# Two-mixer stage of a two-block transformer: row sums as a 129th column, values as weights, attention output in columns

## The chip, the cores and the metric

One core of a Trainium2 chip runs the whole program. The metric is the device time of one execution in microseconds. Engines: PE is TensorE (PEld its weight loads), DVE VectorE, ACT ScalarE, POOL GpSimd, SP SyncE, which here only issues DMAs.

## The reference, cut to what matters

The program computes two transformer blocks on 1024 tokens of width 1024. The change is in the second block, where two mixers run side by side on 8 chunks of 128 tokens: attention over a window of 128 keys (8 heads of 64, 2 key and value heads), and a gated linear recurrence (mlstm, 4 heads of 128).

```python
mx = jnp.maximum(logits.max(axis=-1, keepdims=True), sink)
e = jnp.exp(logits - mx)
p = e / (e.sum(axis=-1, keepdims=True) + jnp.exp(sink - mx))
out = jnp.einsum('bkgnqs,bnskd->bnqkgd', p, vv)          # attention, then
att = rms_norm(out.reshape(b, s, 512), norm_att_out)     # over all 512 columns of a token
...
num = einsum('bhts,bhsd->bhtd', s, v) + a * einsum('bhtk,bhkv->bhtv', q, c_st)
den = s.sum(axis=-1) + a * einsum('bhtk,bhk->bht', q, n_st)
h = num / jnp.maximum(jnp.abs(den), jnp.exp(-m_t))[..., None]
c_new = decay * c_st + einsum('bhsk,bhsv->bhkv', k * w, v)
n_new = decay * n_st + einsum('bhs,bhsk->bhk', w, k)
...
x = x + jnp.concatenate([att, rms_norm(sigmoid(o) * h)], axis=-1) @ w_out
```

## The kernel before, in words

The program is a row of stages, each with its own instruction list per engine, written out by hand and separated by a barrier. `stage_in2` projects the inputs, `stage_mixers` (L1820 to L2270) does both mixers, `stage_residual` multiplies by w_out and adds. Nothing in `stage_mixers` is planned by a scheduler: the order of the calls in each engine's function is the order of its queue, and semaphores join the engines.

`stage_mixers` runs an unrolled loop over 8 blocks i of 128 tokens. PE's part of a block, in its order:

- `h_back(i-1)` (L1999) turns the recurrence's result into columns; `scores(i+1, (0, 1))` (L1895) multiplies queries by keys for four of eight heads.
- `read(i)`: per head two matmuls with a ones column or n_st as the moving operand, 1 column each, for den (L1920, L1921, into bank N), and two with 128 columns for num (L1922, L1923, bank O).
- `memory_project(i-1)` (L1942, L1945): keys and values of the later cross attention, 8 matmuls of 256 columns; it is work of another part of the network, put here.
- `write(i)`: per head a 1-column matmul for the change of n (L1952) and one of 128 columns for the change of the state c (L1953, bank U).
- `scores(i+1, (2, 3))`, then `turn(i)` (L1969): 16 transposes of probabilities in four groups, two banks, each of which DVE copies out (`keep`, L2123) before the third and fourth group.
- `att_back(i-1)` (L1989): 4 transposes of the normed attention rows; `keys(i+1)` (L1909): 4 transposes.
- `weigh(i)` (L1979): probabilities as weights (128x128), values as the moving operand, 64 columns: 16 matmuls. `decays(i+1)` (L1902) ends the block.

Every fp32 matmul shows as two instructions in the trace, a transpose as one. DVE, between its waits, scales the attention rows (L2136), makes m_s (`weights`, L2077), the logits (L2045) and their maxima, `hidden` (L2095 to L2104), the state's update (L2111 to L2116) and `keep`. ACT makes the exponentials (L2190), norms both results (`att_norm`, `h_norm`), and scales by the gains on the way out of the banks (`att_out` L2232, `h_out` L2238):

```python
for h in range(QH):                 # weigh(n), L1979
    kv = h // (QH // 2)
    for r in range(2):
        m = pe.matmul(T[1][:, h * DH:(h + 1) * DH], pt[:, 2 * h + r, :],
                      va[:, n + r, kv * DH:(kv + 1) * DH], start=r == 0, stop=r == 1)
```

SP loads the gate rows of a chunk (L1884), each after an update of the state, and at block 2 the memory rows and both halves of w_ckv (1 MB, 2 MB, 2 MB).

`stage_residual` first loads the stream (4 MB, SP) and then w_out in tiles of 512 KB; ACT (`split_high`, L205) and DVE (`split_low`, L212) split its input into two parts, and `Weights` does so with w_out.

Of the kernel before, what the change touches and what calls it, by code (L numbers as in the profile page):

```python
# [17 lines left out]
ALU = mybir.AluOpType  # L18
# [4 lines left out]
P = 128  # L23
# [30 lines left out]
ML_H = 4  # L54
MEM = 256
# [51 lines left out]
def stage_constants(nc, ctx, A, K, bank):  # L107
# [4 lines left out]
    with ExitStack() as inner:  # L112
# [3 lines left out]
        @block.sync  # L116
        def _(sp):
            sp.wait_ge(rows_zero, 1)
            for name, source, n in VECS:
                a = A[source]  # L120
                v = a.rearrange("o (k p) -> (o k) p", p=P) if len(a.shape) == 2 else a.rearrange("o t (k p) -> (o t k) p", p=P)
                c = VEC[name]
                sp.dma_start(rows[c % P:c % P + n, c // P, :], v).then_inc(rows_in, 16)
            sp.wait_ge(rows_in, 16 * len(VECS))
# [42 lines left out]
        def _(pe):  # L167
            pe.wait_ge(rows_in, 16 * len(VECS))
# [33 lines left out]
def split_high(act, x, xh, made, first=0, end=None):  # L202

    for t in range(first, end or len(x)):
        act.copy(xh[t], x[t]).then_inc(made, 1)  # L205


def split_low(dve, x, xh, xl, hi_made, made):

    for t in range(len(x)):  # L210
        dve.wait_ge(hi_made, t + 1)
        dve.tensor_tensor(xl[t], x[t], xh[t], ALU.subtract).then_inc(made, 1)  # L212


class Weights:
# [4 lines left out]
    def __init__(self, ctx, inner, nc, name, tiles, used):  # L220
# [6 lines left out]
    def load(self, sp, n, s, source):  # L227
        sp.wait_ge(self.lo_made, free(n))
        sp.dma_start(self.raw[:, s, :, :], source).then_inc((self.loaded0, self.loaded1)[s], 16)

    def high(self, act, n, s, round_):
        act.wait_ge((self.loaded0, self.loaded1)[s], 16 * round_ + 16)
# [1293 lines left out]
def stage_in2(nc, ctx, A, K, bank, u, qa, ka, va, qk, vm, og, cols, dist, sinks, rows_d):  # L1526
# [12 lines left out]
    with ExitStack() as inner:  # L1539
# [8 lines left out]
        v_rows, q_rows = vm[0:ML_H, :, :].rearrange("p c n -> p (c n)"), qa[0:ML_H, :, :].rearrange("p k t -> p (k t)")  # L1548
        gi, lf, m_, negm = (v_rows[:, j * SEQ:(j + 1) * SEQ] for j in range(4))
        b, a = (q_rows[:, j * SEQ:(j + 1) * SEQ] for j in range(2))  # L1550
        row2 = q_rows[:, 2 * SEQ:4 * SEQ].rearrange("p (c r t) -> p c r t", r=2, t=P)

# [102 lines left out]
        def _(act):  # L1655
# [19 lines left out]
            def keep_group(n, c):  # L1675
# [5 lines left out]
                else:  # L1681
                    act.copy(vm[:, c, 384:512], out[:, 0:P])
# [51 lines left out]
        def _(dve):  # L1734
# [75 lines left out]
            for c in range(NB):  # L1810
                dve.wait_ge(gmm, NB + c + 1)
                dve.tensor_copy(vm[:, c, 0:384], bank[4 + c % 2][:, 0:384]).then_inc(g_kept, 1)
# [7 lines left out]
def stage_mixers(nc, ctx, A, K, bank, qa, ka, va, qk, vm, og, cols, dist, sinks, rows_d, mk, mv):  # L1820

    (scored, logit, maxed, exped, root, turned, pt_kept, pvmm, small, scaled, ss_made, normed, back, b_kept) = sems(
        ctx, nc, "a", "scored logit maxed exped root turned pt_kept pvmm small scaled ss_made normed back b_kept")
    (bc0, bc1, rm_made, dec, gate_made, fmm, s_made, q_made, kt, kw_made, omm, den_made, hmade, umm, state, nmade,
     hs_made, h2_made, hback, hb_kept, wexp) = sems(
# [1474 lines left out]
```

## Time and profile before

| | |
|---|---|
| median of 3 runs | 3372.41 us (3363.12 to 3375.85) |
| the profiled execution | 3371.22 us, its span 3369.5 us |
| busy share of the span: PE, PEld, DVE, ACT, POOL | 85%, 75%, 48%, 36%, 17% |
| granted PE clock over the span | 0.909 of full speed |
| `stage_mixers` | from about 2025 to 2282 us of the span |

A granted clock of 1.00 is 2.4 GHz, 0.50 is 1.2 GHz; a stretch between them was partly at either level. Busy time of PE and of PEld overlap. A duration of a matmul includes latency, so the pace of a sequence is read from start to start.

### The profile page before, as it was taken

Reading aid. Unit: us, or ns where it says so; the run is one execution under the profiler, and the core shown is the slowest. Engines: PE = TensorE matmul, PEld = TensorE weight load, DVE = VectorE, ACT = ScalarE, POOL = GpSimd, SP = SyncE. Lnnn points to the kernel's source line nnn. Section 1 sums busy time; section 2 is a strip of 40 time slices with the busy share of each in tenths; the row PEclk is TensorE's granted clock in tenths of the full one; section 3 lists DMA queues with packets and bytes.
Section 4 is the critical chain, followed back from the end, with each engine's and each line's share of the span. In section 5 each row is a group of like instructions: output and inputs, shape, how many; then the busy total and the mean of one; then the engine's idle time right before and its main releaser. Section 6 shows DMA issues by size and latency. Waiting matters only on the chain. (4 is left out here: it accounts for less than half of the span.)

```text
span 3369.5 us, 39296 instructions
## 1 busy us (share of the span) xinstructions
PE 2864.1 (85%) x14811; PEld 2515.0 (75%) x14811; DVE 1616.0 (48%) x1956; ACT 1219.2 (36%) x1781; POOL 575.8 (17%) x336
## 2 busy tenths in 40 slices
PE   3889999888499999979939998987677569999992
PEld 2879999788388999867818897775566458888882
DVE  2336655450523323224363415442323369999995
ACT  3324333321311111123233215442221257777773
POOL 2000000003422222101040000002201234444341
PEclk7999999999799999989969997788888589999996
DMA  2332222342121111032211212003001269999995
GB/s 102 107 109 95 95 95 91 113 128 76 50 62 44 50 44 50 25 137 94 94 62 45 46 37 88 19 7 100 25 0 27 119 256 411 407 404 405 405 408 199
DMA packets 223133, 432.17 MB, mean 128 GB/s; under 512 B 21302, under 2 KB 159914, under 8 KB 197690
## 3 DMA queue, kind: packets, MB, share of 16 engines
q1 hardware_dynamic: 213018, 396.21, 32.7%
q0 software_dynamic: 10016, 34.62, 2.6%
q8 instruction: 66, 1.08, 0.1%
q14 instruction: 33, 0.27, 0.0%
HBM read 370.85 MB, written 59.93 MB: 128 GB/s over the span
## 5 line engine op out<-in xcount | busy, mean ns | idle before, releaser
L3050 DVE TENSOR_TENSOR k_w_lo<-k_raw,k_w_hi 128x2048 fp32r<-128x2048 f32 x192 | 435.4, 2291 | 51.0 <-ACT k_w_hi L2996 47.1
L2996 ACT CAST k_w_hi<-k_raw 128x2048 fp32r<-128x2048 f32 x192 | 363.5, 1907 | 94.2 <-PE bank L2916 48.2
L192 PE MATMUL bank<-u_ffn_hi,f_w_hi 128*128 128x342 f32 (+1 forms) x880 | 308.5, 351 | 33.7 <-POOL f_w_lo L1323 33.7
L193 PE MATMUL bank<-u_ffn_lo,f_w_hi 128*128 128x342 f32 (+1 forms) x880 | 308.5, 351 | 0.0
L194 PE MATMUL bank<-u_ffn_hi,f_w_lo 128*128 128x342 f32 (+1 forms) x880 | 308.2, 350 | 0.0
L238 POOL TENSOR_TENSOR wo_w_lo<-wo_w,wo_w_hi 128x1024 fp32r<-128x1024 f32 x16 | 38.3, 2396 | 1371.5 <-ACT wo_w_hi L234 1371.5
L2914 PE MATMUL bank<-k_w_hi,k_x_hi 128*128 128x512 f32 x512 | 206.6, 403 | 5.8 <-DVE k_x_lo L3056 5.6
L192 PEld LDWEIGHTS bank<-u_ffn_hi,f_w_hi 128*128 128x128 f32 x880 | 166.8, 190 | 49.8 <-issue 34.2
L2915 PE MATMUL bank<-k_w_lo,k_x_hi 128*128 128x512 f32 x512 | 203.6, 398 | 0.0
L2916 PE MATMUL bank<-k_w_hi,k_x_lo 128*128 128x512 f32 x512 | 203.3, 397 | 0.0
L192 PE MATMUL bank<-u_hi,g_w_hi 128*128 128x342 f32 (+2 forms) x576 | 190.8, 331 | 13.5 <-DVE g_w_lo L746 10.6
L193 PE MATMUL bank<-u_lo,g_w_hi 128*128 128x342 f32 (+2 forms) x576 | 185.2, 321 | 0.0
L194 PE MATMUL bank<-u_hi,g_w_lo 128*128 128x342 f32 (+2 forms) x576 | 184.2, 320 | 0.0
L194 PEld LDWEIGHTS bank<-u_ffn_hi,f_w_lo 128*128 128x128 f32 x880 | 166.7, 189 | 15.6
L193 PEld LDWEIGHTS bank<-u_ffn_lo,f_w_hi 128*128 128x128 f32 x880 | 166.4, 189 | 15.8
L1323 POOL TENSOR_TENSOR f_w_lo<-f_raw,f_w_hi 128x1024 fp32r<-128x1024 f32 x44 | 105.3, 2395 | 380.9 <-ACT f_w_hi L1349 380.9
L1433 PE MATMUL bank<-d_x_hi,d_w_hi 128*128 128x512 f32 x352 | 138.7, 394 | 23.6 <-DVE d_x_lo L1460 23.3
L1381 DVE TENSOR_SCALAR hidden<-f_gate,vec 128x1024 f32 x22 | 17.9, 812 | 262.0 <-ACT f_gate L1355 262.0
L1434 PE MATMUL bank<-d_x_lo,d_w_hi 128*128 128x512 f32 x352 | 138.3, 393 | 0.0
L1435 PE MATMUL bank<-d_x_hi,d_w_lo 128*128 128x512 f32 x352 | 138.1, 392 | 0.0
L1459 DVE TENSOR_TENSOR d_w_lo<-d_raw,d_w_hi 128x1024 fp32r<-128x1024 f32 x44 | 55.5, 1262 | 169.3 <-ACT d_x_hi L1484 169.3
L192 PEld LDWEIGHTS bank<-u_hi,g_w_hi 128*128 128x128 f32 x576 | 109.3, 190 | 14.1 <-DVE g_w_lo L746 11.0
(538 smaller groups left out, 6982.8 us busy)
## 6 DMA issues: line engine op xcount, KB each, us to landing
k_raw<-in_w_e_gate_dram SPq DMA_DIRECT2D x64, 1024.0 KB, 8.1
k_raw<-in_w_e_up_dram SPq DMA_DIRECT2D x64, 1024.0 KB, 7.5
k_raw<-in_w_e_down_dram SPq DMA_DIRECT2D x64, 1024.0 KB, 8.2
d_raw<-in_ffn_w_down_dram SPq DMA_DIRECT2D x44, 512.0 KB, 3.2
g_w<-in_w_in_dram SPq DMA_DIRECT2D x24, 512.0 KB, 4.3
f_raw<-in_ffn_w_gate_dram SPq DMA_DIRECT2D x22, 512.0 KB, 3.9
f_raw<-in_ffn_w_up_dram SPq DMA_DIRECT2D x22, 512.0 KB, 3.8
gate_scratch<-g_out SPq DMA_DIRECT2D x20, 513.0 KB, 6.3
```

The source lines that it names most:

```text
L192: pe.matmul(out, wh[:, t, :], xh[t][:, c:c + n], start=t == 0, stop=False)
L193: pe.matmul(out, wh[:, t, :], xl[t][:, c:c + n], start=False, stop=False)
L194: m = pe.matmul(out, wl[:, t, :], xh[t][:, c:c + n], start=False, stop=t == tiles - 1)
L1323: pool.tensor_tensor(wl[:, e, :, :], raw[:, e, :, :], wh[:, e, :, :], ALU.subtract).then_inc(lo_made[e], 1)
L1433: pe.matmul(bank[j][:, :], wh[:, s, col], xh[:, s, :], start=first, stop=False)
L1434: pe.matmul(bank[j][:, :], wh[:, s, col], xl[:, s, :], start=False, stop=False)
L1435: m = pe.matmul(bank[j][:, :], wl[:, s, col], xh[:, s, :], start=False, stop=last)
L2914: pe.matmul(out, hi, wh[:, q, col], start=first, stop=False)
L2915: pe.matmul(out, hi, wl[:, q, col], start=False, stop=False)
L2916: return pe.matmul(out, lo, wh[:, q, col], start=False, stop=last)
L2996: act.copy(wh[:, q, :], raw[:, r, :]).then_inc(hi_made, 1)
L3050: dve.tensor_tensor(wl[:, q, :], raw[:, r, :], wh[:, q, :], ALU.subtract).then_inc(lo_made, 1)
```

## The change

It has five parts.

1. **129th column.** `vm` gets 130 columns per head (`VW = P + 2`), the 129th a one, written by POOL at the stage's start. n_st becomes the 129th column of the state. `read` is 8 matmuls of 129 columns (before: 8 of 128 and 8 of one), `write` 4 (before: 4 and 4). The results of heads 0 and 1 lie in bank O, 2 and 3 in N, the state's change of head 3 also in N, so that `write`'s last head waits for `hidden` of the same block.
2. **Values as weights.** `values_wide` holds each value head in its 64 of 128 columns with zeros in the others (POOL: a memset, two copies). `weigh` is 4 matmuls of 512 columns, and its output has head dimensions on partitions and tokens along the free axis: columns, as w_out wants them.
3. **Denominators spread.** They are per token, so `spread_inverse` makes rows of them with 8 matmuls (weights: a denominator column broadcast to 64 columns, moving: ident), after `weigh`, in the scores' bank S[0]. ACT copies the bank (`keep_inverse`), DVE multiplies (`scale`). The next block's first scores wait for the copy.
4. **Norm in columns.** `att_back`, `att_norm` and `att_out` go. ACT squares, PE sums over partitions with ones (`att_sums`, 4 matmuls of 128 columns, between `scores(i+1, (2, 3))` and `turn(i)`), ACT makes the root (`att_root`), DVE multiplies into qa (`place`, one block later).
5. **Moves.** The attention gain is applied in `stage_residual`'s split (mul for copy on ACT, scalar_tensor_tensor for tensor_tensor on DVE); as the heads now pair as j and j + 4, w_out is loaded in 3 DMAs per tile (one for 64 partitions, one for the other 64, one for the rest), norm_att in 2. There is no room for all of w_ckv, so its second half follows in two DMAs of 1 MB, ahead of the gate rows of chunks 4 and 6, behind waits for `memory_project(1)` and `(3)`.

```diff
             def read(c):
...
                 for h in range(ML_H):
-                    pe.matmul(N[:, h:h + 1], sc[:, head(h)], ones[:, 0:1], start=True, stop=False)
-                    pe.matmul(N[:, h:h + 1], qw[:, head(h)], nst[:, h:h + 1], start=False, stop=True)
-                    pe.matmul(O[:, head(h)], sc[:, head(h)], vm[:, c, head(h)], start=True, stop=False)
-                    m = pe.matmul(O[:, head(h)], qw[:, head(h)], st[:, head(h)], start=False, stop=True)
+                    pe.matmul(result(h), sc[:, head(h)], with_sum(c, h), start=True, stop=False)
+                    m = pe.matmul(result(h), qw[:, head(h)], st[:, wide(h)], start=False, stop=True)
...
             def write(c):
                 pe.wait_ge(kw_made, c + 1)
-                pe.wait_ge(den_made, 3 * c + 2)
                 for h in range(ML_H):
-                    pe.matmul(N[:, ML_H + h:ML_H + h + 1], kw[:, head(h)], ones[:, 0:1], start=True, stop=True)
-                    m = pe.matmul(U[:, head(h)], kw[:, head(h)], vm[:, c, head(h)], start=True, stop=True)
+                    if h == ML_H - 1:
+                        pe.wait_ge(hmade, c + 1)
+                    m = pe.matmul(change(h), kw[:, head(h)], with_sum(c, h), start=True, stop=True)
...
             def weigh(n):
                 pe.wait_ge(pt_kept, 4 * n + 4)
-                if n:
-                    pe.wait_ge(b_kept, n)
-                for h in range(QH):
-                    kv = h // (QH // 2)
+                for kv in range(2):
                     for r in range(2):
-                        m = pe.matmul(T[1][:, h * DH:(h + 1) * DH], pt[:, 2 * h + r, :], va[:, n + r, kv * DH:(kv + 1) * DH], start=r == 0, stop=r == 1)
+                        m = pe.matmul(T[1][:, :], vz[:, n + r, kv, :], pt[:, r, kv * 4:kv * 4 + 4, :], start=kv == r == 0, stop=kv == r == 1)
...
+            def spread_inverse(n):
+                pe.wait_ge(small, 2 * n + 2)
+                if n < LAST:
+                    pe.wait_ge(logit, 4 * n + 7)
                 for j in range(4):
+                    for e in range(2):
+                        inverse = den[:, n % 2, 1, 4 * e + j:4 * e + j + 1].to_broadcast([P, DH])
+                        m = pe.matmul(S[0][e * DH:(e + 1) * DH, head(j)], inverse, ident[:, :], start=True, stop=True)
+                m.then_inc(spread, 1)
+
+            def att_sums(n):
+                pe.wait_ge(sq_made, n + 1)
+                pe.wait_ge(kv_kept, n + 1)
+                for j in range(4):
+                    m = pe.matmul(F[:, MEM:MEM + P], ones[:, :], att_sq[:, head(j)], start=j == 0, stop=j == 3)
+                m.then_inc(sums, 1)
...
+            def scale(n):
                 dve.wait_ge(pvmm, n + 1)
+                dve.wait_ge(inverse_kept, n + 1)
...
+                dve.tensor_tensor(att[:, n % 2, :], inverse_row[:, :], T[1][:, :], ALU.mult).then_inc(scaled, 1)
+
+            def place(n):
+                dve.wait_ge(rstd_made, n + 1)
+                dve.tensor_tensor(qa[:, :, chunk(n)], heads(att[:, n % 2, :]), att_r[:, :].unsqueeze(1).to_broadcast([P, 4, P]), ALU.mult).then_inc(placed, 1)
...
+            def keep_inverse(n):
+                act.wait_ge(spread, n + 1)
...
+                act.copy(inverse_row[:, :], S[0][:, :]).then_inc(inverse_kept, 1)
...
     def load(self, sp, n, s, source):
         sp.wait_ge(self.lo_made, free(n))
-        sp.dma_start(self.raw[:, s, :, :], source).then_inc((self.loaded0, self.loaded1)[s], 16)
+        if self.heads:
+            for e in range(2):
+                half = source[0:self.heads * DH, :].rearrange("(j d) n -> d j n", d=DH) if e == 0 else source[self.heads * DH:2 * self.heads * DH, :].rearrange("(j d) n -> d j n", d=DH)
+                sp.dma_start(self.raw[e * DH:(e + 1) * DH, s, 0:self.heads, :], half).then_inc((self.loaded0, self.loaded1)[s], 16)
+            source = source[2 * self.heads * DH:, :].rearrange("(k p) n -> p k n", p=P)
+        sp.dma_start(self.raw[:, s, self.heads:, :], source).then_inc((self.loaded0, self.loaded1)[s], 16)
```

How the order moves, first on PE, from `turn` of a block to the `read` of the next. Before (one row is one kind of matmul, xN its count; att_normed is the normed rows, m_h_normed the recurrence's result, ka and qa keys and queries):

```order
L1969 MATMUL bank<-ident,logits 128x128 x16
L1989 MATMUL bank<-ident,att_normed 128x128 x4
L1909 MATMUL bank<-ident,qk 128x128 x4
L1979 MATMUL bank<-va,probs_t 128x64 x16
L1902 MATMUL bank<-qk 128x128 x4
L1999 MATMUL bank<-ident,m_h_normed 128x128 x4
L1895 MATMUL bank<-ka,qa 128x256 x4
L1920 MATMUL bank<-ones,m_s 128x1
L1921 MATMUL bank<-m_n,m_qw 128x1
L1922 MATMUL bank<-vm,m_s 128x128
L1923 MATMUL bank<-m_c,m_qw 128x128
```

With the change, from `att_sums` on (row_den holds the denominators):

```order
L2046 MATMUL bank<-att_squares,ones 128x128 x4
L2020 MATMUL bank<-ident,logits 128x128 x16
L1959 MATMUL bank<-ident,qk 128x128 x4
L2029 MATMUL bank<-probs_t,values_wide 128x512 x4
L2039 MATMUL bank<-ident,row_den 64x128 x8
L1952 MATMUL bank<-qk 128x128 x4
L2056 MATMUL bank<-ident,m_h_normed 128x128 x4
L1945 MATMUL bank<-ka,qa 128x256 x4
L1971 MATMUL bank<-vm,m_s 128x129
L1972 MATMUL bank<-m_c,m_qw 128x129
```

The 4 transposes of att_normed are gone, 4 sums stand ahead of `turn`, and `spread_inverse` (row_den) stands between `weigh` and `decays`.

Second on DVE, from `keep` to the next logits. Before (m_s is what `read` needs):

```order
L2123 COPY probs_t<-bank 128x512 x4
L2070 SCALAR_TENSOR_TENSOR m_qw<-qk,m_rows 128x512
L2129 TENSOR_TENSOR row_den<-row_den,row_max 128x8
L2131 RECIPROCAL row_den<-row_den 128x8
L2136 TENSOR_TENSOR att_rows<-bank,row_den 128x512
L2077 SCALAR_TENSOR_TENSOR m_s<-m_rows,bank 128x512
```

With the change:

```order
L2183 COPY probs_t<-bank 128x2x2x128 x4
L2128 SCALAR_TENSOR_TENSOR m_qw<-qk,m_rows 128x512
L2189 TENSOR_TENSOR row_den<-row_den,row_max 128x8
L2191 RECIPROCAL row_den<-row_den 128x8
L2203 TENSOR_TENSOR qa<-att_cols,att_rstd 128x4x128
L2199 TENSOR_TENSOR att_cols<-att_inverse,bank 128x512
L2135 SCALAR_TENSOR_TENSOR m_s<-m_rows,bank 128x512
```

`place` of the block before is new ahead of the scaling, and the scaling (att_cols) now reads att_inverse, which ACT copies from PE's spread bank; m_s is made behind it as before.

## Rows read from the trace of the kernel before

**Rows 1.** Page, part 1: busy us of each engine (share of the span) xinstructions.
```profile
PE 2864.1 (85%) x14811; PEld 2515.0 (75%) x14811; DVE 1616.0 (48%) x1956; ACT 1219.2 (36%) x1781; POOL 575.8 (17%) x336
```

**Rows 2.** Windows: stretch, length, busy us by engine, PEclk granted, DMA share, GB/s.
```profile
2024.00:2064.26 40.26, 30.05 (x130) 25.28 (x128) 24.24 (x66) 22.62 (x75) 0.00 (x0) 0.65 0.46 170
2064.26:2265.87 201.61, 182.17 (x1021) 161.52 (x1021) 98.57 (x270) 93.24 (x355) 0.00 (x0) 0.80 0.04 14
2119.86:2155.59 35.73, 33.19 (x149) 29.11 (x149) 15.06 (x41) 14.22 (x56) 0.00 (x0) 0.64 0.05 15
2221.18:2245.81 24.63, 21.43 (x149) 18.79 (x149) 14.97 (x41) 14.11 (x56) 0.00 (x0) 1.00 0.00 1
2265.87:2282.20 16.33, 11.69 (x56) 10.06 (x56) 1.12 (x2) 4.11 (x13) 0.00 (x0) 0.79 0.00 0
```

**Rows 3.** Timeline of PE, one block: start us, us, instruction, count, idle before.
```profile
2221.18 3.75 PE L1979 MATMUL bank<-va,probs_t 128*128 128x64 f32 x32 [0.47 <-ACT qa L2232]
2224.77 1.11 PE L1902 MATMUL bank<-qk 128*128 128x128 f32 x8
2225.71 0.60 PE L1999 MATMUL bank<-ident,m_h_normed 128*128 128x128 f32 x4
...
2228.16 0.38 PE L1920 MATMUL bank<-ones,m_s 128*128 128x1 f32 x2
...
2228.63 0.47 PE L1922 MATMUL bank<-vm,m_s 128*128 128x128 f32 x2
...
2229.16 0.28 PE L1920 MATMUL bank<-ones,m_s 128*128 128x1 f32 x2
...
2231.84 3.62 PE L1945 MATMUL bank<-e_wv,e_mem 128*128 128x256 f32 x16
2235.30 0.28 PE L1952 MATMUL bank<-ones,m_kw 128*128 128x1 f32 x2
2235.43 0.47 PE L1953 MATMUL bank<-vm,m_kw 128*128 128x128 f32 x2
2235.74 0.28 PE L1952 MATMUL bank<-ones,m_kw 128*128 128x1 f32 x2
...
2237.17 1.99 PE L1895 MATMUL bank<-ka,qa 64*128 64x256 f32 x8
2239.09 1.09 PE L1969 MATMUL bank<-ident,logits 128*128 128x128 f32 x8
2242.33 1.25 PE L1969 MATMUL bank<-ident,logits 128*128 128x128 f32 x8 [2.14 <-DVE probs_t L2123]
2243.86 0.63 PE L1989 MATMUL bank<-ident,att_normed 128*128 128x128 f32 x4 [0.28 <-DVE probs_t L2123]
2244.37 0.66 PE L1909 MATMUL bank<-ident,qk 128*128 128x128 f32 x4
2245.81 3.76 PE L1979 MATMUL bank<-va,probs_t 128*128 128x64 f32 x32 [0.79 <-ACT qa L2232]
```

**Rows 4.** Timeline of PE: four instructions of 512 columns, fp32, a later stage.
```profile
2397.80 3.49 PE L2312 MATMUL bank<-wo_acc,ones 128*128 128x512 f32 x4 [5.01 <-POOL wo_acc L2375]
```

**Rows 5.** Windows: pieces at the lower level, and two in which it ends.
```profile
2185.64:2192.48 6.84, 6.84 (x32) 6.84 (x33) 0.00 (x0) 0.88 (x4) 0.00 (x0) 0.50 0.00 0
2217.23:2220.64 3.41, 3.39 (x16) 2.52 (x14) 2.55 (x6) 2.04 (x10) 0.00 (x0) 0.50 0.00 0
2270.40:2274.70 4.30, 4.30 (x11) 3.48 (x12) 0.69 (x1) 0.00 (x0) 0.00 (x0) 0.50 0.00 0
2274.70:2276.30 1.60, 1.60 (x7) 1.27 (x6) 0.00 (x0) 0.00 (x0) 0.00 (x0) 0.83 0.00 0
```

**Rows 6.** Timeline of DVE: the scaling of the attention output by its denominators.
```profile
2225.02 0.69 DVE L2136 TENSOR_TENSOR att_rows<-bank,row_den 128x512 f32<-128x512 f32 x1 [4.64 <-PE bank L1979]
```

**Rows 7.** Timeline of ACT, a later stage: a copy of one bank.
```profile
2538.66 0.59 ACT L2529 COPY co<-bank 128x512 f32 x1 [5.17 <-PE bank L2476]
```

**Rows 8.** Timeline of PE: first matmul of the projection that follows.
```profile
2301.27 0.80 PE L192 MATMUL bank<-wo_x_hi,wo_w_hi 128*128 128x512 f32 x1 [20.55 <-POOL wo_w_lo L238]
```

More of the change, by code:

```diff
@@ L54 @@
 ML_H = 4
+VW = P + 2
 MEM = 256
@@ L1870, in head, with wide, result, change @@
             return slice(h * P, (h + 1) * P)
+        def wide(h):
+            return slice(h * VW, h * VW + P + 1)
+        def result(h):
+            return (O, N)[h // 2][:, h % 2 * VW:h % 2 * VW + P + 1]
+        def change(h):
+            return U[:, h * VW:h * VW + P + 1] if h < ML_H - 1 else N[:, 2 * VW:2 * VW + P + 1]
+        def with_sum(c, h):
+            return vm[:, (c * ML_H + h) * VW:(c * ML_H + h) * VW + P + 1]
         def chunk(c):
@@ L1884, in _ @@
                 sp.dma_start(bc[:, c % 2, :, :], rows_d[c:c + 1, :, :, :].rearrange("a r h t -> a r (h t)").to_broadcast([P, 2, BANK])).then_inc(bc_in[c % 2], 16)
+        @block.gpsimd
+        def _(pool):
+            ones_column = vm[:, :].rearrange("p (c h t) -> p c h t", c=NB, h=ML_H)[:, :, :, P:P + 1]
+            pool.memset(ones_column, 1.0).then_inc(v_ones, 1)
+            pool.memset(vz[:, :, :, :], 0.0).then_inc(v_wide, 1)
+            pool.wait_ge(v_wide, 1)
+            for kv in range(2):
+                half = slice(kv * DH, (kv + 1) * DH)
+                pool.tensor_copy(vz[:, :, kv, half], va[:, :, half]).then_inc(v_wide, 1)
         @block.tensor
@@ L2019, in _ @@
                     memory_turn(2)
+                if i:
+                    att_sums(i - 1)
                 turn(i)
-                if i:
-                    att_back(i - 1)
                 if i < LAST:
@@ L2025, in _ @@
                 weigh(i)
+                spread_inverse(i)
                 if i == 0:
@@ L2032, in _ @@
             h_back(LAST)
-            att_back(LAST)
+            att_sums(LAST)
         @block.vector
@@ L2167, in _ @@
                 finish(i)
+                if i:
+                    place(i - 1)
+                scale(i)
                 if i == 0:
@@ L2172, in _ @@
             memory_store(LAST)
+            place(LAST)
         @block.scalar
@@ L2227, in keys @@
                 x.then_inc(kw_made, 1)
-            def att_out(n):
-                act.wait_ge(back, n + 1)
-                for j in range(4):
-                    x = act.mul(qa[:, j, chunk(n)], T[1][:, j * P:(j + 1) * P], vec[:, VEC["norm_att"] + j:VEC["norm_att"] + j + 1])
-                x.then_inc(b_kept, 1)
             def h_out(c):
@@ L2291, in _ @@
                 for s in range(2):
-                    wt.load(sp, 2 * i + s, s, w[:, :, ds((2 * i + s) * P, P)])
+                    at = ds((2 * i + s) * P, P)
+                    wt.load(sp, 2 * i + s, s, weights[:, at] if gains else w[:, :, at])
         @block.tensor
@@ L3255, in program @@
                 mixed = [qa[:, j, :] for j in range(4)] + [qk[:, j, :] for j in range(4)]
-                stage_residual(nc, ctx, A, K, bank, "wo2", A["w_out_2"][0], KD, mixed, h, qk, "norm_cross", h_load=h2_d)
+                stage_residual(nc, ctx, A, K, bank, "wo2", A["w_out_2"][0], KD, mixed, h, qk, "norm_cross", h_load=h2_d,
+                               gains=[K["vec"][:, VEC["norm_att"] + j:VEC["norm_att"] + j + 1] for j in range(4)])
             with ExitStack() as cross:
```

173 lines of the change are left out of this document (97 added, 76 removed).

## The prediction, made before the changed kernel had run

> **What bounds the kernel now.** I read the page first: PE is busy for 85% of the span [rows 1], so a change inside one stage is worth what it does to PE's path in that stage. Then the stage in windows [rows 2]. The reader is to see two things. PE is busy in 182.2 of the 201.6 us from the first `weigh` to the last, DVE and ACT in under half: PE bounds the stage. And the granted clock over those 201.6 us is 0.80, so 2 x 0.20 x 201.6 = 81 us were at the lower of the two levels. A block with the same instructions takes 24.63 us at 1.00 and 35.73 us at 0.64. With all blocks at full clock the stretch would take 6 x 24.63 us and a last block of 20.1 us (it has no scores; it too ran at 1.00), 167.8 us. So the lower level costs 33.8 us of 201.6, that is 0.42 us for each us spent there.
>
> Third, the timeline of one block at full clock [rows 3]. PE waits in it at two places. In the middle of `turn` it is idle for 2.14 us until DVE has copied a bank (DVE is late with the state's update, logits and maxima), and 0.79 us before `weigh`, which waits for ACT's `att_out`. From the end of the scores to the start of `weigh`, 6.7 us, it does only transposes and waits. In the 1-column and 64-column pieces it is paced by weight loads: 32 `weigh` instructions of 64 columns take 3.59 us start to start, 0.112 us each, and 8 of `decays` with 128 columns take 0.94 us, 0.118 us each. Half the columns cost nearly the same.
>
> **The change, part by part, in a block at full clock.**
>
> *`read`.* It takes 3.68 us, from 2228.16 to 2231.84 [rows 3]. What stays is 16 instructions of 129 columns. At the pace of `decays` that is 16 x 0.118 = 1.88 us; at the pace that the 128-column ones have inside `read`, 0.53 us for four, it is 2.1 us. I take the first, since the new sequence is like `decays`: -1.8 us (bounds -1.6 and -1.8).
>
> *`write`.* 1.87 us now, from 2235.30 to 2237.17. 8 instructions at 0.118 us are 0.94 us; at the pace of a pair of L1953 (0.31 us) 1.24 us. I take -0.93 us (bound -0.6). The new wait of its last head for `hidden` costs nothing: `memory_project` runs for 3.46 us between `read` and `write` and `hidden` needs about 2 (six small operations and four of 128 columns). Without that cover PE would stand for up to 2 us, and the scores and `turn` behind it.
>
> *`weigh`.* 8 instructions of 512 columns. `memory_project` has 16 of 256 columns in 3.46 us, 0.216 us each, so 8 x 0.43 = 3.46 us against 3.59: -0.13 us. At the lower level four such instructions take 3.49 us [rows 4] (a stretch nearly all at that level), eight 7.0 us, against 6.84 us for the old form [rows 5]. The row says that this half of the change is worth nothing by itself, because 64-column instructions were paced by their weights. The Trainium skill, "TensorE: Matmul & The Clock Gate", section Back-to-back issue gap, has the gap of a matmul proportional to its columns down to a small floor. By it alone the zero-padded form, 2048 columns for 1024, would double `weigh`, +1.7 us per block; the trace does not agree, since 64 columns take 0.112 us where 128 take 0.118 us.
>
> *`att_back` and the wait behind it.* From the start of `att_back` (2243.86) to the next `weigh` (2245.81) are 1.95 us. Now `keys` follows `turn` once DVE's last copy is done, about 0.6 us after 2243.86, and takes 0.5 us, and `weigh` follows at once: -0.86 us. If a copy is late by as much as ACT was, it is 0.
>
> *`att_sums`.* 8 instructions of 128 columns, 0.94 us, between the scores and `turn`. They fall into the 2.14 us for which `turn` waits for DVE anyway, so they cost 0; if that wait were gone, 0.94 us. DVE's way from the end of `write` to its first copy is 5.2 us and stays (three operations of about 0.16 us less).
>
> *`spread_inverse`.* 16 instructions of 128 columns, weights of 64 columns, before `decays`, with nothing to hide it. No row shows weights of 64 columns or two that lie in different halves of the array. At the pace of `decays` 16 x 0.118 = 1.88 us; if the halves ran beside each other 0.94 us. I take +1.88 us, the nearest row.
>
> *The round trip behind it.* DVE can scale only after the spread and ACT's copy (0.59 us [rows 7]), then 0.69 us [rows 6] and as much again for m_s: about 2.4 us after the spread with hand-overs. PE meanwhile has `decays` 0.94, `h_back` 0.5 and four heads of scores 1.9 us, 3.4 us before `read` needs m_s. Cost 0 at full clock, with 1 us to spare; at the lower level PE's cover doubles. What is late next is DVE's `hidden`, by about 1 us, and `memory_project` covers that.
>
> *ACT and DVE.* ACT loses four gain operations and four of the norm and gets a copy, a square and two operations on 128 columns; DVE gets one more of 0.69 us. Both have 10 us free in a block. 0.
>
> Sum per block: -1.8 - 0.93 - 0.13 - 0.86 + 1.88 = -1.84 us, 22.8 us in place of 24.6. Seven blocks: **-12.9 us**.
>
> **The clock.** This is the larger term. The level falls behind the 6.7 us of `turn`, idling and transposes, in five of seven blocks, and then stays low for long. At the lower level 6.84 us of `weigh` in 64-column pieces, PE busy throughout, did not end it [rows 5]. It ended behind 256-column `memory_project` (4.3 us of it from 2270.40, and the window from 2274.70 is already at 0.83 [rows 5]), or behind dense transposes (the window from 2217.23 [rows 5], with 1.00 right after it [rows 2]). With the change the weak stretch shortens to 1.0 (`turn`) + 1.2 (idle left over) + 2.7, 4.9 us, with real matmuls ahead of it, and what follows it is 7 us of 512-column `weigh`. I expect the level still to fall in most blocks, and to come back inside `weigh`, some 5 us later: 5 x 5 = 25 us low in place of 81. At 0.42 us each that is 10.3 in place of 33.8: **-23.5 us**.
>
> **The ends of the stage.** In block 0 (clock 0.65 [rows 2]) `read` and `write` at the lower level save twice their terms, 5.5 us, part of it lost to waits for DVE: -4 us. The tail, 16.3 us at 0.79: `weigh` the same, the spread added, the last normalisation with fewer steps on ACT (one square, two small ones, no second pass) but sums on PE: -1 us. Start: POOL's memset and copies run beside DVE's first logits, and `stage_residual` now gets its first w_out tile in three DMAs. PE stands there for 20.6 us behind a 4 MB load [rows 8], so a later first tile is on the path; norm_att has a DMA more. Together +1 us (0 to 3). The later loads of w_ckv have two blocks before they are used, and the gate rows behind them nearly one: 0. The gain in the split is one operation for one: 0.
>
> **Sum**: -12.9 - 23.5 - 4 - 1 + 1 = -40.4 us. From 3371.2 us of the profiled execution that gives 3330.8; the median of the runs shown is 1.2 us above it: **3332 us**.
>
> **The rivals.**
>
> 1. *The clock stays as low as before.* The fixed savings remain, -12.9 - 4 - 1 + 1 us and about 2 more because they are larger at the lower level: 3353 us. For it: `turn` and its idling stay, and the level has outlasted most of a block (35.73 us at 0.64 [rows 2]). Against it: wide streams ended it each time they ran for 4 us. 0.15.
> 2. *Transposes do not hold the clock.* The weak stretch then reaches from the scores to `weigh` in every block: seven falls, 35 us low, +4 us: 3336 us. Against it [rows 5], window 2217.23: 3.4 us of nothing but transposes at the lower level, and the block behind them ran at 1.00 from its start. The Trainium skill, same page, section Part 4: PE-mode transpose, says that they don't count as activity and the clock doesn't rise in them; here it did. 0.12.
> 3. *It never falls.* The leftover idling is too short. All blocks at 22.8 us: -51 us, and if the two halves of the spread run together -6.6 more: 3320 to 3314 us. For it: the block at 2221.18 kept 1.00 through the same 2.14 us of idling. 0.15.
> 4. *The round trip becomes the bound, slower than before.* Place: DVE's `scale` waits for spread and copy, and m_s, the logits and ACT's exponentials are queued behind it. It decides once it outlasts the 3.4 us of PE work that cover it by more than what is saved, 41 us over 8 blocks, 5 us a block. That takes a spread several times dearer than any row (broadcast weights are the one thing here that no row shows). At 7 us more a block: 3332 + 56 = 3388 us. 0.04.
>
> **How the numbers follow.** My forecast has 0.54. The range runs from rival 3 to just beyond rival 1, 3314 to 3357 us; it takes in the unknown price of the spread (+-0.9 us in eight blocks, 7 us) and of the start. About 0.5%, 17 us, is what a measurement of this kernel can tell from no change, so "faster" ends at 3355.5 us. Forecast, rivals 2 and 3 lie clear of it, rival 1 with some two thirds: 0.54 + 0.12 + 0.15 + 0.09 = 0.90, less 0.02 for what I have not seen, 0.88; same 0.07; slower 0.05.
>
> **What would show it.** In the profile after: `read` at 1.9 us and `write` at 0.94 us at full clock; `weigh` at 3.5 us in 8 instructions; the idling in `turn` at about 1.2 us; the spread at 1.9 us; no wait of PE for m_s; a mean clock over the seven blocks of 0.9 or more, with low stretches that end inside `weigh`. Wrong it would be if PE waits behind the spread for DVE or ACT, if the low stretches outlast `weigh`, or if w_out's first tile lands microseconds later.

## The result, and the profile after

The changed kernel takes **3311.9 us** (median of 4 runs, 3308.65 to 3315.98) against 3374.1 before in the same session: ratio 0.9819, 95% interval 0.9802 to 0.9836. It is 62 us faster, where 40 were forecast (3332 us, range 3314 to 3357): right in sign, outside the range by 2 us. The profiled execution took 3310.0 us, its span is 3308.3 us. The page's first part (answers to [rows 1]):

```profile
PE 2809.9 (85%) x14587; PEld 2444.1 (74%) x14587; DVE 1619.6 (49%) x1963; ACT 1210.2 (37%) x1741; POOL 590.2 (18%) x340
```

PE's share is the same 85%: its work went down with the span. The stage in windows (answers to [rows 2]; columns as there): from the stage's start to the first `weigh`, from there to the last, one block at full clock, the block in which the level fell, the last block, the tail (its window ends 0.4 us before `place` is done).

```profile
2024.00:2056.53 32.53, 20.78 (x109) 16.66 (x108) 24.09 (x65) 22.52 (x75) 3.35 (x4) 0.86 0.41 146
2056.53:2209.97 153.44, 139.85 (x825) 105.70 (x824) 100.73 (x275) 84.95 (x320) 0.00 (x0) 0.97 0.10 32
2147.12:2169.13 22.01, 20.02 (x122) 15.30 (x121) 15.45 (x44) 12.97 (x49) 0.00 (x0) 1.00 0.08 25
2169.13:2191.57 22.44, 20.45 (x123) 15.73 (x121) 15.82 (x46) 12.98 (x49) 0.00 (x0) 0.98 0.00 1
2191.57:2209.97 18.40, 16.74 (x101) 12.33 (x100) 7.86 (x22) 7.12 (x26) 0.00 (x0) 0.94 0.00 0
2209.97:2222.80 12.83, 9.97 (x52) 6.71 (x52) 2.36 (x6) 2.92 (x8) 0.00 (x0) 1.00 0.00 1
```

The reader is to see three numbers. The seven blocks take 153.44 us, before 201.61. Their granted clock is 0.97, before 0.80. And a block at full clock takes 22.01 us, before 24.63. Of the 61.2 us by which the span shrank, 48.2 lie in these seven blocks. The way to the first `weigh` gives 8.4 (it starts 7.7 us earlier in a stage that starts 0.7 later), from the last `weigh` to the first matmul of the projection 2.5 (35.4 us, now 32.9), and what follows 2.8. None of those 2.8 us lie in the projection, which the change does touch (96.5 us from its first matmul to that of the next stage before, 96.6 now); they lie in the cross attention, in code that the change does not touch.

One block at full clock on PE (answers to [rows 3]; start us, us, instruction, count, idle before):

```profile
2147.12 3.60 PE L2029 MATMUL bank<-probs_t,values_wide 128*128 128x512 f32 x8
2150.65 1.09 PE L2039 MATMUL bank<-ident,row_den 128*64 128x128 f32 x16
2151.67 1.16 PE L1952 MATMUL bank<-qk 128*128 128x128 f32 x8
...
2155.12 0.49 PE L1971 MATMUL bank<-vm,m_s 128*128 128x129 f32 x2
...
2157.01 3.62 PE L1996 MATMUL bank<-e_wk,e_mem 128*128 128x256 f32 x16
2160.46 1.05 PE L2004 MATMUL bank<-vm,m_kw 128*128 128x129 f32 x8
2161.45 1.99 PE L1945 MATMUL bank<-ka,qa 64*128 64x256 f32 x8
2163.37 1.16 PE L2046 MATMUL bank<-att_squares,ones 128*128 128x128 f32 x8
2164.36 1.04 PE L2020 MATMUL bank<-ident,logits 128*128 128x128 f32 x8
2166.60 1.25 PE L2020 MATMUL bank<-ident,logits 128*128 128x128 f32 x8 [1.20 <-DVE probs_t L2183]
2168.64 0.66 PE L1959 MATMUL bank<-ident,qk 128*128 128x128 f32 x4 [0.79 <-DVE probs_t L2183]
2169.13 3.60 PE L2029 MATMUL bank<-probs_t,values_wide 128*128 128x512 f32 x8
```

Start to start, against before:

| piece | before | after | forecast |
|---|---|---|---|
| `weigh` | 3.59 | 3.53 (2147.12 to 2150.65) | -0.13 |
| `spread_inverse` | none | 1.02 (to 2151.67) | +1.88 |
| `decays`, `h_back`, scores | 3.39 | 3.45 (to 2155.12) | 0 |
| `read` | 3.68 | 1.89 (to 2157.01) | -1.8 |
| `write` | 1.87 | 0.99 (2160.46 to 2161.45) | -0.93 |
| `write`'s end to the third group of `turn` | 5.16 | 5.15 (2161.45 to 2166.60) | 0 |
| from there to `weigh` | 3.48 | 2.53 (to 2169.13) | -0.86 |
| block | 24.63 | 22.01 | -1.84 |

`att_sums` (2163.37, 0.99 us) lies in the gap as forecast: `turn` now waits 1.20 us for DVE in place of 2.14. The round trip behind the spread on ACT and DVE (answers to [rows 6, 7]):

```profile
2151.79 0.58 ACT L2267 COPY att_inverse<-bank 128x512 f32<-128x512 f32 x1 [3.33 <-PE bank L2039]
...
2152.47 0.69 DVE L2199 TENSOR_TENSOR att_cols<-att_inverse,bank 128x512 f32<-128x512 f32 x1 [4.25 <-ACT att_inverse L2267]
2153.07 0.68 DVE L2135 SCALAR_TENSOR_TENSOR m_s<-m_rows,bank 128x512 f32<-128x512 f32 x1
```

m_s is made by 2153.75 and `read` starts at 2155.12: 1.4 us to spare, where I had worked out 1.

### The profile page after: what moved, and what is told of

It reads as the page before. It is cut to its first block and busy times, and to the rows that moved or that the text cites. A ratio compares the mean times of both kernels' runs of the same rounds, so it can differ in the third digit from the quotient of the medians.

```text
span 3308.3 us, 38889 instructions
## 1 busy us (share of the span) xinstructions
PE 2809.9 (85%) x14587; PEld 2444.1 (74%) x14587; DVE 1619.6 (49%) x1963; ACT 1210.2 (37%) x1741; POOL 590.2 (18%) x340
## 5 line engine op out<-in xcount | busy, mean ns | idle before, releaser
L198 PE MATMUL bank<-u_hi,g_w_hi 128*128 128x342 f32 (+2 forms) x576 | 191.7, 333 | 13.8 <-DVE g_w_lo L765 10.8
```

The source lines that it names most:

```text
L198: pe.matmul(out, wh[:, t, :], xh[t][:, c:c + n], start=t == 0, stop=False)
```

## The experiments

Two questions were open. Why does the level hardly fall any more, and how much of the gain is clock and how much is work? Eleven kernels ran, each beside the kernel before, whose median was 3374 to 3377 us; the ratios are to that one. The low time is 2 x (1 - PEclk) x length of the window from the first `weigh` to the last; as PEclk has two digits, it is known to within 2 us (9 and 6 us in the table are not different). Windows and falls are read from one execution of each kernel, and executions of one kernel differ: part 1 alone took 3323.6 to 3334.8 us, of which the profile shows the slowest, and `weigh` in 64 columns 3348.1 to 3352.6 us and, in the one profiled, 3361.8.

| run | median us | ratio to before (95%) | seven blocks us, clock, low us | a block at full clock us |
|---|---|---|---|---|
| before | 3374 | | 201.6, 0.80, 81 | 24.63 |
| changed | 3311.9 | 0.9819 (0.9802 to 0.9836) | 153.4, 0.97, 9 | 22.01 |
| before + filler | 3344.7 | 0.9918 (0.9894 to 0.9942) | 181.7, 0.92, 29 | 24.64 |
| before + 129th column | 3329.7 | 0.9864 (0.9842 to 0.9886) | 171.9, 0.83, 58 | 22.02 |
| before + 129th column + filler | 3321.4 | 0.9833 (0.9814 to 0.9852) | 161.4, 0.92, 26 | 21.95 |
| changed without 129th column | 3340.3 | 0.9899 (0.9880 to 0.9918) | 174.8, 0.96, 14 | 24.96 (at 0.99) |
| changed, `weigh` in 64 columns | 3351.5 | 0.9931 (0.9912 to 0.9950) | 199.1, 0.87, 52 | 25.67 |
| changed, `weigh` in 128 columns | 3315.0 | 0.9835 (0.9811 to 0.9859) | 154.2, 0.98, 6 | 22.15 |
| changed, sums behind `turn` | 3316.6 | 0.9829 (0.9810 to 0.9847) | 158.6, 0.93, 22 | 22.69 (at 0.97) |
| changed, spread half by half | 3317.2 | 0.9834 (0.9816 to 0.9853) | 161.9, 0.94, 19 | 22.50 |
| changed, `keep` first | 3301.0 | 0.9789 (0.9770 to 0.9809) | 146.3, 0.99, 3 | 21.16 |
| before + 129th column, `keep` first | 3350.0 | 0.9923 (0.9903 to 0.9942) | 192.3, 0.80, 77 | none |
| before, `keep` first | 3371.8 | 0.9981 (0.9968 to 0.9994) | 204.2, 0.85, 61 | none |

### Filling the gap of the kernel before

```diff
+            def filler(n):
+                pe.wait_ge(kv_kept, n)
+                for j in range(4):
+                    m = pe.matmul(F[:, MEM:MEM + P], ones[:, :], ident[:, :], start=j == 0, stop=j == 3)
...
+                if i:
+                    filler(i)
                 turn(i)
```

> The kernel before, with four idle matmuls of 128 columns (ones by ident, written to columns of bank F that nobody reads; the output does not depend on them) ahead of turn in blocks 1 to 7: 0.94 us of matmul in the 2.14 us for which turn waits for DVE. Theory A (the clock falls because of the long stretch of waits and transposes from the scores to weigh, and matmuls in it hold the level): the mean granted clock from the first to the last weigh rises from 0.80 to 0.93 or more, most blocks take 24.6 to 25.5 us, the time falls by 20 to 32 us though work was added: 3342 to 3354 us. Theory B (the level is kept by the wide streams of weigh and by read without 1-column pieces, not by what stands in the gap): the clock stays at 0.75 to 0.85 and the time within 8 us of 3374.

Theory A held: 29 us less for work that was added, 19.9 of them in the seven blocks (201.61 to 181.68 us); the rest lies behind the last `weigh`. The windows of the seven blocks, of one block at full clock and of the one in which the level fell:

```profile
2064.35:2246.03 181.68, 165.73 (x1077) 147.01 (x1077) 98.26 (x270) 93.28 (x355) 0.00 (x0) 0.92 0.05 15
2143.76:2168.40 24.64, 22.38 (x157) 19.72 (x157) 14.97 (x41) 14.14 (x56) 0.00 (x0) 1.00 0.06 23
2168.40:2201.18 32.78, 30.52 (x156) 26.79 (x157) 14.97 (x41) 14.24 (x56) 0.00 (x0) 0.74 0.05 17
```

A block at full clock is as long as before (24.64 us): the 8 instructions cost nothing, since `turn` waits 1.20 us instead of 2.14, as it does in the changed kernel. Behind block 0 the level falls once in place of five times. The low stretch that block 0 leaves, which has no filler, is as long as before (37.6 us, to 2075.3). The one fall is not explained by the gap: `turn` and `keys` in front of it ran at full clock, and so did the first 2.4 us of `weigh`, up to 2170.8; the level was then low for 17.1 us. Why in this block and not in its neighbours, no run tells.

### Part 1 alone, and parts 2 to 5 alone

Part 1 alone is the kernel before with the changed `read`, `write`, `hidden`, `update` and layout of vm. The other kernel is the changed one with these undone, so that `read` and `write` have their 1-column matmuls again.

> The kernel before with part 1 alone (row sums as a 129th column in read and write; weigh, att_back and the norm as before). Both theories: read 1.8 to 2.1 us and write about 1 us at full clock, a block at full clock 24.6 - 2.8 = 21.9 us. Theory A: the clock still falls behind turn in most blocks, mean 0.75 to 0.85, since the stretch from the scores to weigh is untouched; the saving is 2.8 us a block at full clock and up to 5 at the lower level, about 28 us: 3340 to 3352 us. Theory B: denser read lets the level come back before memory_project, mean 0.86 or more, and the time falls by 35 us or more.

> The changed kernel with part 1 undone: 1-column and 128-column matmuls in read and write as before, parts 2 to 5 as changed. Full clock: 22.0 + 2.8 = 24.8 us a block, so as many us as before, 24.6. Theory A with wide weigh: the level falls seldom and comes back inside weigh, low time under 25 us of seven blocks, 3334 to 3346 us: parts 2 to 5 are worth nothing at full clock and 28 to 40 us by the clock alone. If the clock needs the denser read too: 3350 us or more.

Seven blocks, one with a fall, one at full clock: first part 1 alone, then parts 2 to 5 alone.

```profile
2060.20:2232.10 171.90, 152.51 (x853) 133.32 (x853) 98.16 (x271) 93.19 (x355) 0.00 (x0) 0.83 0.05 16
2110.54:2138.06 27.52, 24.91 (x124) 21.65 (x125) 14.96 (x41) 14.14 (x56) 0.00 (x0) 0.75 0.05 20
2192.85:2214.87 22.02, 18.82 (x125) 16.16 (x125) 14.88 (x41) 14.14 (x56) 0.00 (x0) 1.00 0.00 0
```

```profile
2063.48:2238.32 174.84, 161.25 (x994) 126.03 (x993) 101.45 (x275) 85.36 (x320) 0.00 (x0) 0.96 0.08 28
2166.01:2192.02 26.01, 24.02 (x146) 18.47 (x145) 15.25 (x41) 13.04 (x49) 0.00 (x0) 0.95 0.06 21
2192.02:2216.98 24.96, 22.97 (x146) 18.27 (x145) 15.80 (x45) 13.04 (x49) 0.00 (x0) 0.99 0.00 1
```

Part 1 alone gives 46 us by its ratio, far more than the 28 of theory A. The block at full clock is 22.02 us, that of the whole change, and the level still falls in most blocks as A said. 27.52 us at 0.75 are 13.8 us low; the block of [rows 2] at 0.64 had 25.7. Theory B was right in the time, though not in the clock (0.83, where it wanted 0.86 or more). Of the 29.7 us that the seven blocks are shorter here, 18.3 are work (seven times 2.61), the rest clock. That a denser `read` by itself shortens a low stretch is likely but not shown. The kernel before had short ones too, as in the block behind that of [rows 2], 13.2 us low:

```profile
2155.59:2185.64 30.05, 27.17 (x149) 24.24 (x149) 14.98 (x41) 14.13 (x56) 0.00 (x0) 0.78 0.05 19
```

And in the last of the experiments low stretches last 10.2 us each time with the old `read` and 10.2 to 20.5 us with the dense one.

Parts 2 to 5 alone give 34 us, as expected, though their block at (nearly) full clock, 24.96 us at 0.99, is no shorter than before's 24.63. **At full clock the values as weights, the spread and the new norm are worth nothing; all they give is clock.** The block with a fall, 26.01 us at 0.95, has 2.6 us of low time. The two halves together (46 + 34 us by their ratios) exceed the whole (61). In the seven blocks they give 29.7 and 26.8 us for 48.2: the low level cost 33.8 us there, and both win part of the same.

### Part 1 with the filler

The edit is both of the above together.

> The kernel before with part 1 (129th column) and the four idle matmuls ahead of turn in blocks 1 to 7 (as in the first of these runs; nobody reads them). e2_columns alone has a full-clock block of 22.0 us, as the whole change has, but 58 us of low time. Theory A: with the gap filled the level holds in most blocks: low time under 25 us of seven blocks, 3310 to 3325 us, so that part 1 and a filler give all or most of what the whole change gives. If parts 2 to 5 bring something of their own beside the clock: 3330 us or more.

```profile
2060.30:2221.65 161.35, 145.40 (x909) 126.67 (x909) 97.67 (x270) 93.03 (x355) 0.00 (x0) 0.92 0.05 17
2109.76:2138.25 28.49, 26.23 (x133) 22.50 (x133) 14.96 (x41) 14.12 (x56) 0.00 (x0) 0.76 0.05 20
```

3321.4 us, as theory A had it: two additions to the kernel before, one of them idle work, give 56 of 61 us by the ratios. What is missing against the whole change is in the windows. When the level does fall, it stays low for 13.7 us (28.49 us at 0.76), in the changed kernel for 3 (22.44 at 0.98 and 18.40 at 0.94 are the two windows that its one fall straddles).

### How wide the pieces of `weigh` must be

```diff
-                for kv in range(2):
-                    for r in range(2):
-                        m = pe.matmul(T[1][:, :], vz[:, n + r, kv, :], pt[:, r, kv * 4:kv * 4 + 4, :], ...)
+                for x in range(8):
+                    for kv in range(2):
+                        for r in range(2):
+                            piece = pt[:, r, kv * 4 + x * 64 // P, x * 64 % P:x * 64 % P + 64]
+                            m = pe.matmul(T[1][:, x * 64:(x + 1) * 64], vz[:, n + r, kv, :], piece, ...)
```

The second run has 4 pieces of 128 columns in place of 8 of 64.

> The changed kernel with weigh cut into 32 matmuls of 64 columns (64 instructions in place of 8 of 512), the kind of stream that the kernel before had, and twice as many. Each at 0.112 us: weigh takes 7.2 us at full clock in place of 3.46, +3.7 us a block, +30 us. Theory A: the clock holds as in the changed kernel (mean 0.95 or more over the seven blocks): 3340 to 3346 us. Theory B: the level falls and is not brought back inside weigh, mean 0.85 or less, 3360 us or more.

> The changed kernel with weigh cut into 16 matmuls of 128 columns (32 instructions at 0.118 us, 3.8 us for 3.46, +0.3 us a block, +3 us by itself). It tells whether the width of the pieces matters for the clock beyond 128 columns. If 128-column streams bring the level back as 512-column ones do: low time as in the changed kernel, up to 15 us, 3313 to 3320 us. If not, low stretches that outlast weigh as in the 64-column run (17 us each there): 3325 us or more.

In pieces of 64 (seven blocks, one with a fall, one at full clock), then `weigh` at full clock; in pieces of 128 the seven blocks:

```profile
2059.01:2258.15 199.14, 185.56 (x1217) 167.76 (x1216) 100.96 (x275) 85.04 (x320) 0.00 (x0) 0.87 0.07 25
2126.52:2160.24 33.72, 31.73 (x178) 28.92 (x177) 15.54 (x44) 12.99 (x49) 0.00 (x0) 0.75 0.05 16
2185.92:2211.59 25.67, 23.68 (x178) 21.08 (x177) 15.47 (x44) 12.98 (x49) 0.00 (x0) 1.00 0.07 22
```

```profile
2185.91 7.26 PE L2031 MATMUL bank<-probs_t,values_wide 128*128 128x64 f32 x64
2193.10 1.09 PE L2041 MATMUL bank<-ident,row_den 128*64 128x128 f32 x16
```

```profile
2056.77:2211.01 154.24, 140.64 (x994) 123.13 (x993) 100.79 (x275) 85.01 (x320) 0.00 (x0) 0.98 0.10 32
```

In pieces of 64 both theories are half right. The level holds in the last four blocks (three of 25.67 us, 22.01 + 3.7 as forecast, and the last, which has no scores), with 7.2 us of such streams in each. But in the first three it is low for 17 us each (33.72 at 0.75), past the end of `weigh`. Pieces of 128 do as well as 512: 6 us low, and 0.14 us more a block. So narrow streams kept the level as long as PE was busy, and did not bring it back.

The windows of all thirteen kernels say the same of the length. Behind block 0, where a low stretch reached into `weigh` by more than 0.2 us, it lasted 3.4 us each time with pieces of 128 or 512 columns (11 times in five kernels), and 10.2 to 27.3 us with 64 columns (22 times in seven kernels). How long it stays low hangs on the width of what follows; whether it falls hangs in the main on the gap, as the filler and the next section show, but not on it alone.

### The order of the sums

```diff
-                if i:
-                    att_sums(i - 1)
                 turn(i)
+                if i:
+                    att_sums(i - 1)
```

> The changed kernel with att_sums behind turn, where att_back stood, in place of ahead of it. The same instructions, in another order: turn's wait for DVE is 2.1 us again and the 0.94 us of sums lie on PE's path, though they now fill the 0.79 us for which keys waits for DVE's last copy. Full-clock cost +0.2 to +1.0 us a block, 1 to 7 us. Theory A (the level falls because of what stands between the scores and weigh): the level falls again in several blocks, the low time of the seven blocks rises from 7.7 us to 20 or more; but by theory A2 (e5: how long it stays low is set by the streams that follow) each low stretch stays short, 3 to 7 us, because weigh is wide. Together 3316 to 3330 us. If the order of the sums is of no matter: 3312 to 3316.

```profile
2059.31:2217.88 158.57, 144.24 (x825) 112.18 (x824) 101.07 (x275) 83.24 (x318) 0.00 (x0) 0.93 0.09 31
2108.25:2131.77 23.52, 21.38 (x122) 16.91 (x121) 15.57 (x42) 13.07 (x51) 0.00 (x0) 0.93 0.06 23
```

As expected by A: five falls, each short (23.52 us at 0.93: 3.3 us), 22 us low in all. Of the six blocks with scores none ran wholly at full clock. The reason that the expectation gives for their being short, the wide `weigh`, is not the whole one: three of the five were over when `weigh` began (low from 2104.5 to 2107.9, `weigh` at 2108.25), with only transposes and the sums in the low stretch. The cost is 4.7 us by the medians, which are of two sessions; the intervals of the two ratios overlap, so the time alone does not show it, the count of falls does.

This run also tells how far block 0 can be trusted. Up to the first `weigh` its instructions are those of the changed kernel, and yet that stretch took 35.31 us at 0.67 here and 32.53 us at 0.86 there.

### The two halves of the spread

```diff
-                for j in range(4):
-                    for e in range(2):
+                for e in range(2):
+                    for j in range(4):
```

> The changed kernel with the loops of spread_inverse exchanged: four matmuls into the lower 64 output partitions, then four into the upper 64, so that neighbours no longer lie in different halves of the array. If halves that alternate run beside each other (which would explain 1.02 us for 16 instructions), the sequence takes 1.7 to 1.9 us and the time rises by 5 to 8 us, to 3317 to 3320. If instructions with 64 columns of weights are simply cheaper (paced by a shorter load), nothing changes: 1.0 us, 3312 within 3.

The spread in the timeline of PE, at full clock:

```profile
2181.05 1.58 PE L2039 MATMUL bank<-ident,row_den 128*64 128x128 f32 x16
2182.56 1.16 PE L1952 MATMUL bank<-qk 128*128 128x128 f32 x8
```

Neither expectation of the sequence was right alone. 16 instructions take 1.51 us, 0.094 each, where neighbours lie in the same half; 1.02 us, 0.064 each, where the halves alternate; `decays` with 128 columns of weights has 0.118. So the narrower weights give about half of the gain over `decays`, and the alternation the rest. The time rose by 5 us, of which 0.49 us a block are 4. The level fell in four blocks behind block 0 in place of one (19 us low for 9), although nothing changed between the scores and `weigh`. So the same gap can lose the level in one kernel and keep it in another. A shift of the blocks in time may decide; that was not tested.

### Taking the idling away

```diff
                 logits(i + 1, (2, 3))
-                maxima(i + 1, 1)
...
                 keep(i)
+                if i < LAST:
+                    maxima(i + 1, 1)
```

This edit of DVE's order was put into the changed kernel, the kernel before, and the kernel before with part 1.

> The changed kernel with DVE's keep ahead of the maxima of the next block's second half, so that turn no longer waits for three operations of 1.6 us. If turn's 1.2 us and keys' 0.8 us of waiting are on PE's path: a block takes 21.0 to 21.3 us in place of 22.0, the low time stays under 10 us, 3303 to 3307 us. Rival: the exponentials start 2.7 us later on ACT, keep_inverse is queued behind them, and the gain is given back as a wait of PE for m_s: 3309 to 3314 us.

> The kernel before with part 1 and with DVE's keep ahead of the maxima, no filler, no other part: turn's wait of 2.1 us mostly goes, so the gap is closed by taking the idling away in place of filling it. The wait of weigh for ACT's att_out stays. Full clock: 22.0 - 1.7 = 20.3 to 21.0 us a block. Theory A: the level falls in half the blocks at most, 3300 to 3318 us. If ACT's att_out is late behind the exponentials, weigh waits for it longer and the gain is given back: 3325 us or more.

> The kernel before with nothing but DVE's keep ahead of the maxima. Full clock: 24.6 - 1.7 = 22.9 us a block, 12 us in all, and by theory A fewer and shorter low stretches, another 10 to 25 us: 3337 to 3352 us. Without an effect on the clock: 3358 to 3364 us.

The changed kernel with it: seven blocks and one, then `turn`'s third group and `keys` in the timeline of PE.

```profile
2055.63:2201.91 146.28, 137.81 (x827) 104.78 (x825) 102.62 (x282) 86.21 (x329) 0.00 (x0) 0.99 0.10 33
2142.35:2163.51 21.16, 20.03 (x123) 15.31 (x121) 15.46 (x43) 12.84 (x49) 0.00 (x0) 1.00 0.07 26
```

```profile
2097.49 1.26 PE L2020 MATMUL bank<-ident,logits 128*128 128x128 f32 x8 [0.35 <-DVE probs_t L2183]
2099.53 0.66 PE L1959 MATMUL bank<-ident,qk 128*128 128x128 f32 x4 [0.78 <-DVE probs_t L2183]
```

The wait falls from 1.20 to 0.35 us, a block takes 21.16 us, the level does not fall behind block 0, and the kernel takes **3301.0 us** (3299.2 to 3305.4), below all runs of the changed kernel (3308.65 at least) and below both expectations. ACT's later exponentials hurt nobody there.

In the kernel before the same edit is worth about 6 us (2 to 11 by its interval), and with part 1 it undoes 20 us of that gain. Both miss what was expected (3337 to 3352 or, without the clock, 3358 to 3364 us for the one, measured 3371.8; 3300 to 3318 us for the other, measured 3350.0). The seven blocks and one of them, and the row of `weigh` in the same block, of part 1 with `keep` first:

```profile
2057.43:2249.75 192.32, 160.12 (x855) 140.95 (x853) 98.67 (x277) 94.35 (x364) 0.00 (x0) 0.80 0.04 14
2171.09:2199.50 28.41, 23.47 (x124) 20.64 (x125) 14.78 (x41) 13.99 (x55) 0.00 (x0) 0.80 0.06 20
```

```profile
2171.09 7.06 PE L1997 MATMUL bank<-va,probs_t 128*128 128x64 f32 x32 [4.24 <-ACT qa L2252]
```

`weigh` now waits 4.24 us for ACT's `att_out`, where it waited 0.79: the exponentials, started later, stand ahead of it in ACT's queue. My expectation had named this as what could give the gain back. In the kernel before with the same edit, where I had not named it, the wait is the same, 4.25 us, and it made the seven blocks longer (204.2 us for 201.6) though they had less low time (61 us for 81):

```profile
2180.75:2211.44 30.69, 25.75 (x148) 23.08 (x149) 14.89 (x41) 13.98 (x55) 0.00 (x0) 0.83 0.06 19
```

So the one thing that parts 3 and 4 give at full clock is an option: with `att_out` gone from `weigh`'s way, DVE's order can be changed. The clock says the same as the filler run, from the other side: with 4.2 us of idling ahead of a narrow `weigh` the level is low in every block.

## Why the prediction was right or wrong

*What bounds the kernel.* Right. PE bounds the stage, and the low level cost 33.8 us there; the filler run won 19.9 of them with no work removed (29 us in the whole kernel).

*The terms of a block.* `read`, `write`, the way from `turn` to `weigh`, `att_sums` in the gap and the free round trip came out within 0.1 us of the numbers in the table. `weigh` was right too: twice the columns in the same time. The formula of the Trainium skill ("TensorE: Matmul & The Clock Gate", Back-to-back issue gap), proportional to columns, would have had +1.7 us by my estimate. I read it too narrowly: the section gives it for an isolated matmul and says that in a stream of weight loads and matmuls both set the pace, so that it counts too little where there are few columns. With that the runs agree in kind (0.112 us at 64 columns, 0.118 at 128). **`spread_inverse` was mis-sized**: 1.02 us, not 1.88. I took the nearest row and kept 0.94 as a bound; the runs put it near the bound, by narrow weights and by alternating halves. With it the block is 2.6 us shorter, not 1.84. For seven blocks at full clock that makes -18.4 us (167.8 before; six of 22.01 and a last one of 17.4, as in the run with pieces of 128, make 149.4), where -12.9 stood: the spread's size makes these 5.5 us of the miss.

*The clock.* **The step that failed is "I expect the level still to fall in most blocks".** It fell in one block behind block 0, and the low stretch was short, 3 us. The rest of the 48.2 us, 29.8, is the clock term (forecast -23.5). I had the right two causes, the shortened gap and the wide `weigh`, but gave the first no effect on how often the level falls. The run with the sums behind `turn`, which leaves the gap idle and keeps the wide `weigh`, is what I had forecast: five falls, all short. With the sums in the gap there was one. I had also taken all five falls before for long ones; two were over in 3.4 us, before `weigh` began (the window from 2217.23 in [rows 5] is one). Rival 3, the level that never falls, at 0.15, was nearly what happened, and its low end with the halves running together, 3314, was 2 us above the median. That it comes so near is partly luck: the level did fall once, the halves run together only in part, and block 0, the tail and the code behind gave more than it counted.

*Block 0* gave 8.4 us for -4. From the stage's start to the first `weigh` 28 us were low before (0.65 of 40.26 us) and 9 now (0.86 of 32.53). I had counted what `read` and `write` save at the lower level, not that it ends sooner. But whether it does is not the change's alone: the kernel with the sums behind `turn` took 35.31 us for the same instructions, and would have given 5. *The tail* was mis-sized: from the last `weigh` to the first split of `stage_residual` it gave 2.8 us for -1, as the lower level, 6.8 us of it before, is gone. *The start* went as forecast: the stage begins 0.7 us later, and the projection's first matmul comes 0.3 us later behind the split (forecast +1). The 2.8 us behind the projection's start lie in the cross attention (87.4 us, now 84.2), whose instructions are the same and whose clock goes back and forth: in the profiles of nine of the kernels it took 83.8 to 88.0 us. I don't count it as the change's.

*The rivals.* Rival 1 (clock as before) fell. Rival 2 fell too: `turn` and `keys` are all transposes, and the level fell behind them once in seven blocks. The Trainium skill (same page, Part 4: PE-mode transpose) says that the full rate does not engage in transposes, as they do not count as PE being busy in the same way. Had they not held the clock here, the level would have fallen in every block; the trace does not agree. Rival 4 needed a spread several times dearer than any row; it was cheaper.

## What to carry to other kernels

Where TensorE's clock is low in part of a stage, price the idling before the work. Look for the wait behind which the level falls and fill it, or take it away: four matmuls that nobody reads, put into a wait, gave 29 us in a kernel whose work was otherwise untouched. Narrow matmuls cost twice here: 64 columns take nearly as long as 128 (0.112 us an instruction for 0.118), and they leave the level low for 10 us or more after it has fallen, where pieces of 128 columns or more had 3. And where two forms cost the same at full clock, ask which of them frees an order: moving one group of copies ahead won 11 us with the whole change and lost 20 with part 1 alone.

## What the runs showed that I had not expected

- Matmuls whose outputs lie in alternating halves of the partitions follow each other faster: 0.064 us an instruction alternating, 0.094 one half after the other, 0.118 with 128 columns of weights (128 columns moving, fp32, full clock).
- Streams of 64 columns with PE busy throughout keep the high level as well as wide ones do (7.2 us of them in a block at 1.00), but in a block at 0.75 the lower level outlasted them.
- A low level that met `weigh` lasted 3.4 us with pieces of 128 or more columns and either `read`, 10.2 to 20.5 us with 64 columns and the dense `read`, and 10.2 to 27.3 with both narrow (30.69 us at 0.83, 35.73 at 0.64).
- The same instructions can lose the level in one kernel and keep it in another: up to the first `weigh` at 0.86 and at 0.67, and from the scores to `weigh` once in seven blocks and, with the spread half by half, four times in seven.
